# Transposing the keys of a bidirectional retention layer with DMAs instead of TensorE

## The reference, cut to what matters

```python
def step(state, xs):
    qb, kb, vb = xs
    scores = jnp.einsum('bhid,bhjd->bhij', qb, kb) * decay_intra[None]
    intra = jnp.einsum('bhij,bhjv->bhiv', scores, vb)
    inter = jnp.einsum('bhid,bhdv->bhiv', qb, state) * xi[None, :, :, None]
    new_state = state * gamma_c[None, :, None, None] + jnp.einsum(
        'bhjd,bhjv->bhdv', kb * zeta[None, :, :, None], vb)
    return new_state, intra + inter
...
y_fwd = chunkwise_retention(q, k, v, log_gf, include_diag=True)
y_bwd = jnp.flip(chunkwise_retention(jnp.flip(q, 2), jnp.flip(k, 2), jnp.flip(v, 2),
                                     log_gb, include_diag=False), 2)
```

## Time and profile before

| | us |
|---|---|
| three runs | 3898.72, 4215.73 (median), 4425.74 |
| the profiled execution | 3895.36 |
| its span on the slowest core (core 7) | 3893.8 |
| spans of the eight cores | 3873.7 to 3893.8 |
| granted TensorE clock, mean of a core | 0.991 to 0.994 of full speed |

### The profile page before, as it was taken

One profiled execution on the slowest core, in us unless ns is written; L12 is line 12 of the kernel. 1 busy time (PEld: TensorE's weight loads), 2 busy tenths in 40 slices (PEclk: granted clock), 3 DMA queues, 4 the chain that ended last, 5 costly groups with the idle time before them and its releaser, 6 DMA issues.

```text
span 3893.8 us, 61566 instructions; the slowest of 8 cores (3873.7 to 3893.8 us)
## 1 busy us (share of the span) xinstructions
PE 3756.5 (96%) x20960; PEld 1852.3 (48%) x20960; DVE 1687.1 (43%) x2414; ACT 1616.3 (42%) x2799; POOL 1056.9 (27%) x934
## 2 busy tenths in 40 slices
PE   5899999999999999999999999999999899999999
PEld 2444444444445665444444444444444466644444
DVE  3756763222253435222367656632223534442224
ACT  3444452211147885123345444421112598831114
POOL 0544530332123110112354444301122431021111
PEclk9999999999999999999999999999999999999999
DMA  8232349532252232323472232682123422322212
GB/s 175 56 69 55 65 70 195 95 76 31 35 98 50 40 57 42 60 65 87 83 188 55 52 68 50 130 179 38 28 44 52 91 41 42 48 42 42 44 22 87
DMA packets 354641, 277.34 MB, mean 71 GB/s; under 512 B 209056, under 2 KB 305568, under 8 KB 354336
## 3 DMA queue, kind: packets, MB, share of 16 engines
q0 software_dynamic: 96032, 111.16, 18.8%
q1 hardware_dynamic: 258304, 162.25, 16.5%
HBM read 297.48 MB, written 37.75 MB: 86 GB/s over the span
## 4 chain that ended last, share of the span: by engine, by line
PE 85%; DVE 4%; DMA 4%; ACT 3%; issue 3%; POOL 1%; DVEq 0%; ACTq 0%; SPq 0%; POOLq 0%
PE psall L310 84%; ACT sb_M L326 2%; DMA sb_uT<-sb_U 1%; PE psall L316 1%; DVE sb_M L330 1%; POOL sb_M L330 1%; DVE sb_M L342 1%; DVE sb_U L342 1%; DMA sb_M<-yg_scr 1%; ACT sb_st L326 1%; DMA sb_ring<-ret_w_in 1%; ACT sb_U L326 0%; DVE sb_M L336 0%; DMA sb_uT<-sb_M 0%; DMA sb_C<-at_scr 0%
## 5 line engine op out<-in xcount | busy, mean ns | idle before, releaser
L326 ACT ACTIVATE sb_M<-psall 128x512 f32<-128x512 f32 (+2 forms) x1232 | 937.5, 774 | 1415.6 <-PE psall L310 1313.3
L330 POOL TENSOR_TENSOR sb_M<-sb_M 128x512 bf16<-128x512 f32 (+3 forms) x752 | 845.9, 1140 | 1483.3 <-ACT sb_M L326 866.7
L310 PE MATMUL psall<-sb_ring,sb_M 128*128 128x512 bf16 x5120 | 1117.6, 380 | 3.9 <-DMA sb_M<-yg_scr 3.9
L310 PE MATMUL psall<-sb_uT,sb_ring 128*128 128x512 bf16 x5120 | 1112.2, 379 | 0.0
L310 PE MATMUL psall<-sb_ring,sb_uT 128*128 128x512 bf16 x3328 | 847.3, 384 | 10.9 <-DMA sb_ring<-ret_w_in 8.3
L310 PEld LDWEIGHTS psall<-sb_ring,sb_M 128*128 128x128 bf16 x5120 | 501.8, 98 | 608.8 <-issue 12.8
L310 PEld LDWEIGHTS psall<-sb_uT,sb_ring 128*128 128x128 bf16 x5120 | 500.8, 98 | 602.1 <-issue 1.6
L330 DVE TENSOR_TENSOR sb_M<-sb_M,psall 128x1024 f32<-128x1024 f32 (+1 forms) x352 | 394.9, 1123 | 614.1 <-PE psall L310 588.1
L310 PE MATMUL psall<-sb_M 128*128 128x129 bf16 (+2 forms) x5504 | 624.5, 256 | 26.6 <-DVE sb_M L336 13.0
L310 PEld LDWEIGHTS psall<-sb_M 128*128 128x128 bf16 x5504 | 412.3, 97 | 293.2 <-issue 56.2
L310 PEld LDWEIGHTS psall<-sb_ring,sb_uT 128*128 128x128 bf16 x3328 | 322.7, 99 | 328.2 <-issue 29.4
(11 more groups left out here) (43 smaller groups left out, 1179.1 us busy)
## 6 DMA issues: line engine op xcount, KB each, us to landing
sb_ring<-mlp_w POOLq DMA_DIRECT2D x64, 1024.0 KB, 12.6
sb_M<-x SPq DMA_DIRECT2D x80, 512.0 KB, 6.0
sb_ring<-ret_w_in POOLq DMA_DIRECT2D x16, 1024.0 KB, 11.5
yg_scr<-sb_M SPq DMA_DIRECT2D x64, 256.0 KB, 2.2
y<-sb_M SPq DMA_DIRECT2D x32, 512.0 KB, 3.1
sb_ring<-ret_w_in POOLq DMA_DIRECT2D x16, 512.0 KB, 9.5
sb_M<-cos_r SPq DMA_DIRECT2D x32, 256.0 KB, 3.8
sb_M<-sin_r SPq DMA_DIRECT2D x32, 256.0 KB, 4.1
```

The source lines that it names most:

```text
L310: self.S.op("pe", lambda e: e.matmul(out.ap, lhsT.ap, rhs.ap, start=start, stop=stop, **kw), reads=_k(lhsT, rhs), writes=_k(out))
L326: return e.activation(out.ap, in_.ap, func, scale=_a(scale), **kw)
L330: self.S.op(eng, lambda e: e.tensor_tensor(out.ap, in0.ap, in1.ap, op=op), reads=_k(in0, in1), writes=_k(out))
```

## The change

`ktr` no longer uses TensorE or PSUM. Two transposing DMAs on SP, one for each half m, read 128 x 256 of `kT` and write [tokens, 2 chunks, 128] into a new SBUF tile `KN` with two buffers, by b % 2. ScalarE makes the same scaled copies as before, in the same order and at the same place of its list, now from `KN`.

```diff
@@ -676,6 +676,7 @@
         SF = M(39936, [2, 2, 512], BF16)
         ADT = M(44032, [2, 2, 256], BF16)
         QX = M(46080, [2, 2, 2, 256], BF16)
+        KN = M(54272, [2, 2, 2, 128], BF16)
         YGN = M(50176, [4, 512], BF16)
         tabc = [0]
         TP = Pool(B, TFs)
@@ -788,20 +789,16 @@
 
         def ktr(h, b):
 
-            bk = B.bank()
-            pb = PSb(bk)
+            kn = KN.v(b % 2)
+            for m in range(2):
+                B.dma_tr(V(KN.v(b % 2, None, m).ap, KN.v(b % 2, None, m).keys), kT.v(m, (b * 256, (b + 1) * 256)),
+                         key=("kt", b % 2, m))
             for j in range(2):
-                for m in range(2):
-                    c = 2 * b + j
-                    B.tr(V(pb[:, j * 256 + m * 128:j * 256 + (m + 1) * 128], [("ps", bk)]),
-                         kT.v(m, (c * 128, (c + 1) * 128)), ident)
-            for j in range(2):
-                pv = V(pb[:, j * 256:(j + 1) * 256], [("ps", bk)])
+                pv = V(kn.ap[:, j].rearrange("p a b -> p (a b)"), kn.keys)
                 if b > 0:
                     B.act(KZB.v(b % 2, j), pv, AF.Copy, scale=zcol.v(h % 2, (2 + j, 3 + j)))
                 if b < 7:
                     B.act(KZF.v(2 * b + j), pv, AF.Copy, scale=zcol.v(h % 2, (j, j + 1)))
-            B.give(bk)
 
         def state(kz, c0, old, new, gcol):
             for m in range(2):
```

## The result

The changed kernel took 3940.05 us in the median of four runs (3937.54 to 4411.51), the kernel before 4057.22 in the median of the four runs beside it. (The ratio is that of the times, after to before.) The profiled execution took 3942.08 us with a span of 3940.3 on core 7, 46.5 more than before; the cores' spans are 3915.4 to 3940.3.

A forecast was written before the change was run, and what follows sets the result against it. It took PE, busy for 96% of the span, as the bound; -1.5 + 4.4 + 8.4 + 6 = +17.3 us on the profiled 3895.36 gave a forecast of 3912 us, with a range of 3881 to 3950.

The forecast's parts named there:

- rival at 3940: Value stage's start, seven heads: the weight load also delays b = 7's second DMA, at most half the heads; chance 0.15.
- The other rivals: Whole kernel: transposes come off PE whole, 3884 (0.16); two `KN` buffers become the loop, 4050 (0.06); faster, 3795 (0.03).
- a wait before b = 7: Value stage's start, seven heads: a PE wait there, listed as a sign that the forecast is wrong; no size given.
- No gain from blocks 6 to 2, 1 and 0: Value stages of seven heads: removed transposes gain nothing in these blocks, as PE then waits for ScalarE; 0 us.
- Block 7's 1.5 us: Block 7 of seven heads: removed transposes gain 0.22 us each, 1.5 us, if its DMAs are in time.
- ScalarE's reads of SBUF (+4.4): Scaled copies before KZB 1: each 0.035 us slower from SBUF than from PSUM, 4.4 us in all.
- The load at the stage's start (+8.4): Seven value stages: b = 6's DMAs, beside the weight load, land 1.2 us late each, 8.4 us; b = 7 in time.
- The rule that I took for the landing: Value stage's start: b = 6's DMAs land as the load's packets end, 241.6 + some 0.6, 1.2 us late.
- The first head (+6): First head: new DMAs stand behind `tab_load(0)` in SP's list, so its states come late; 6 us taken.
- the 14 of the bounds: First head's upper bound: 4.4 us lost plus 9.9 if b = 0's DMA lands in 12.4 us beside a weight load.
- The chain of `tab_load(0)`: First head: DMAs issue from 111.4 behind that table load; b = 7's state 6.9 us late, b = 6's update 7.0.
- The packet-by-packet turns: DMA engines alternate between queues: 17 waits of 0.065 us, 1.1 us in all, so b = 6 in time, sum 8.4 less.

The follow-up runs named there:

- e_kn4: The changed kernel with four buffers of `KN` in place of two, nothing else different; 3934.87 us.
- e_no_tr: The kernel before with neither transposes nor new DMAs, ScalarE's copies reading `kT` untransposed; ratio to before 0.9973.
- e_late: The changed kernel, first head's DMAs of b = 7 and 6 ahead of `tab_load(0)`, both value-stage weight loads behind POOL's three multiplications in all heads; ratio to before 1.0014.
- e_load13: The changed kernel; in the seven heads the weight load at the value stage's start waits for the cast of chunk 13; ratio to before 1.0085.
- e_13_ahead: e_late with scaled copies ahead of the cast, e_load13's place of the load, and the stage-end load at its old place; ratio to before 1.0001.
- e_all_end: The changed kernel, stage-start weight loads held to block 0's copies in all heads, first head's DMAs of blocks 7 and 6 ahead of `tab_load(0)`; 3917.32 us.

## Why the prediction was wrong

The range held the time, but the move was 45 us and not 17, by the mechanism that stood there as a rival at 3940. That its number came so near is in part luck: it had half of the heads hit at 7.2 us each and nothing else changed. Measured, all seven heads were hit on all eight cores (1.2 to 8.4 us each), the first head cost 9 us more than forecast, and the slow clock behind the waits made 9 us over the whole span, part of them in the first head. The other rivals are out: the period is 4.56 us and not 4.32, four buffers (e_kn4) bring nothing, and the time did not fall. Of the signs that were named, a wait before b = 7 stood under "wrong", and that is what came. Term by term, in the slowest core's trace:

- **No gain from blocks 6 to 2, 1 and 0: right.** Period 4.56 us, wait at the stage's end up by 0.51; e_no_tr shows it with the transposes gone altogether. Block 7's 1.5 us depended on its DMAs being in time, and they were not.
- **ScalarE's reads of SBUF (+4.4): over-sized.** Four copies take 1.71 us where they took 1.58, but the period grew by 0.02, so 0.02 x 42 = 0.8 us. The state's second matmul started 242.27 + 0.22 - 241.06 = 1.43 us behind the copies' start before and 275.43 + 0.22 + 0.24 - 274.44 = 1.45 after. The third copy does end 0.10 us later behind the first's start (1.31 against 1.21), as the 3 x 0.035 had it; but before, the weight load that waits for it stood 0.10 us ahead of its matmul and now 0.03, so KZB 1 lay ready a little early before, where I had it arrive just then.
- **The load at the stage's start (+8.4): this step failed.** It said that b = 7's packets are out before the load's, by the earlier trace rows, since a load's packets start 1.6 us behind its issue. But that holds for the first DMA alone. The second is issued 0.34 us behind the load, its own packets start 1.7 us behind its issue, and in the trace the load's first packet is at 249.47 and the second DMA's at 249.71. It landed at 258.6, 10.6 us on, 0.8 us behind the load's first half. That hits b = 7, whose DMA has under 2 us of slack (at 1.23 us of wait it took 5.3 us to land, so from 4.1 on PE waits, and alone it takes 2.3), where I had put the whole loss before b = 6. Seven waits of 1.23 to 7.39 us, 27.4 in sum on the slowest core (1.67 us in the second head on core 5, 6.55 on core 7); before b = 6 they sum to 1.8. The rule that I took for the landing, with the end of the load's packets, held for b = 6 (its second DMA landed at 261.7, the load's second half at 261.5), but that end came later than in before: 12.9 us after the second half's issue in place of 8.7. This core is an extreme in that: over the eight cores the median is 9.9 in place of 9.6 in the second head, and 9.3 and 9.8 in place of 7.4 and 7.3 in the fifth and sixth.
- **The first head (+6): mis-sized.** Its end came 15.2 us late, beyond even the 14 of the bounds. The chain of `tab_load(0)` was right up to SP's issue (111.74 for 111.4), but the first two landed after 3.1 and 3.7 us in place of 2.5, b = 7's state was 9.3 us late where 6.9 were worked out, and I then let the read-ahead win too much of it back. The load behind b = 1's DMAs (8.77 us of wait) stood in the bounds only and should have been in the sum, for it is the collision of the other seven heads again.
- **The fifth head: a term that was left out.** It opens the second sequence, and its keys come late. Before, PE already waited for POOL's keys there:

```profile
2034.39 0.22 PE L316 MATMUL psall<-sb_st,sb_M 128*128 128x128 bf16 x1 [1.24 <-POOL sb_M L330]
2035.50 0.33 PE L316 MATMUL psall<-sb_st,sb_M 128*128 128x128 bf16 x3 [0.90 <-POOL sb_M L330]
```

and after:

```profile
2072.33 1.86 PE L310 MATMUL psall<-sb_M 128*128 128x512 bf16 x4 [7.39 <-ACT sb_M L326]
```

PE stops at 2064.94, 0.8 us ahead of the second DMA's issue at 2065.75; that lands 5.7 us on and the copies take the rest. So this wait is the longest of the seven on every core (7.1 to 8.4), with a landing like the others' (5.4 to 6.5 us). Without a load beside it (e_late) 4.1 to 4.2 us stay there on seven cores, against the 2.1 of before.

- **Not in the sum at all: the clock after a long wait.** Matmuls whose successor starts 0.40 to 0.45 us later, counted over the span, make some 23 us of lost pace before and some 32 after: 9 us.

The ledger of the slowest core: +46.0 waits for the copies, +9 slow clock, +8 for KZB 1 (35 x 0.24, each too short for the view of waits), -14.1 transposes: 48.9, against 46.5 of span. That is rougher than it looks, for PE's other waits moved too, by up to 4 us a row: all of PE's waits over 0.15 us together grew by 40.4 us (128.7 to 169.1), and with that the sum is 43.

The Trainium skill (DMA: Bandwidth & Descriptors, Issuing engines are not separate DMA queues) says that DMAs of all issuing engines end up on the same 16 engines and interleave there. The trace agrees: between 250.5 and 251.0 us 121 packets of the load and 58 of SP's queue start, and both sides pay, the DMA 2.3 to 10.6 us and the load's second half 7.4 to 9.3 (fifth head, median of the cores). The packet-by-packet turns, which I had priced at 1.1 us in all with the profile's packets of 0.5 KB, it does not bear out for the landing; whether those are the packets that the page speaks of, no run shows. Of the clock the Trainium skill (TensorE: Matmul & The Clock Gate, Part 1) says that an idle array falls back to half rate and gives 426.7 and 215.7 ns between starts of matmuls with 512 columns; the trace agrees (granted clock 0.50 behind the wait, and a value matmul each 0.43 us against 0.216).

Two things stay open. The mean over cores in the first head of the DMA versions stays 3 us above before. And the same DMA, issued 0.2 to 0.4 us behind the load (0.86 once), lands after 5.3 us in one head and 10.6 in another: it goes with how long the load takes (its first half 5.9 to 10.2 us), but what makes the load itself vary, as it does in before too (5.5 to 9.4 us in the second head), was not found.

## What to carry to other kernels

Work that leaves the busiest engine is worth something only if the engine that hands it its operands can come sooner: read what stands ahead of the hand-over in that one's list, and move it together with the change. A new small DMA is priced by its landing beside the large transfer that starts nearest to it, and this at the place with the least slack; moving the large one costs issue time on its own engine, so look at what is behind it there. And a wait of several us on TensorE costs more than its length, since the clock comes back late.

## What the runs showed of the hardware

- A transposing DMA of 128x256 from SBUF to SBUF occupies SP for 1.16 us and lands in 2.3 us alone; issued up to 0.3 us ahead of a 1 MB weight load it took mostly 4.7 to 5.5 (3.8 to 6.8; e_load13 and e_13_ahead), 0.2 to 5 us behind the load's issue 5.3 to 11.4, and 7 to 9 us behind it 3.3 in the median (after, eight cores). SP's own issue was then stretched as well, from 1.16 to 2.5 and 3.2 us in after's second head.
- The load pays too: its second half landed after 9.3 and 9.8 us in the fifth and sixth head where before had 7.4 and 7.3 (medians of the cores).
- Behind a wait of 6.55 us TensorE's granted clock was 0.50 for 5.6 us; behind e_load13's wait of 1.84 us (with one of 0.42 next to it) it was 0.67 in the mean of the next 5.1 us.
- ScalarE's read of a bf16 tile of 128x256 from SBUF takes 0.43 us in a row of four (1.71), from PSUM 0.39 (1.56 to 1.58).
- Issuing a weight load of two halves takes GpSimd 1.81 us, in which it does nothing else; a multiplication behind it came late and TensorE waited 1.93 us (e_all_end).
